# Decode attention on Trainium2: key-page products moved from VectorE to GpSimd, in place

## The chip, the cores and the metric

The kernel runs on one core of one Trainium2 chip. The metric is device time in microseconds (us) of one execution; lower is better. Engines are named as the profile names them: PE is TensorE's matmul, PEld its weight load, DVE is VectorE, ACT is ScalarE, POOL is GpSimd, and SP is SyncE, which here only issues transfers.

## The reference, cut to what matters

One decoder step of two layers over 512 prompt tokens and 8 sample tokens. Layer 0 is a recurrent mixer with a convolutional FFN, layer 1 differential attention with a convolutional FFN. The change is in layer 1's attention of the samples over their paged cache: each of 8 samples has 4 pages of 128 past keys, each key 1024 numbers (8 heads x 2 halves x 64).

```python
qs, ks, vs = att_project(hs, att_w_in[j], att_q_norm_g[j], att_k_norm_g[j])
past_k = cache_k[j, page_table].reshape(db_, past, A_HEADS, 2, A_QK_DIM)
past_v = cache_v[j, page_table].reshape(db_, past, A_HEADS, A_V_DIM)
...
s = jnp.einsum('bqhcd,bkhcd->bchqk', q, k) * A_QK_DIM ** -0.5   # q.k for each key, head and half
p = softmax(s); a = p[:, 0] - lam * p[:, 1]; out = a @ v
```

## The kernel before, in words

Everything is in one program. Each engine has its own block of instructions in an order written out by hand, and the engines meet only at semaphores: `Steps` (a named list of counts) turns the name of a step and a round number into a wait.

Layer 1's attention is done in 8 rounds of `head(h, ...)`, one such function on each of PE, ACT, DVE and POOL. Rounds 0 and 7 are written out, rounds 1 to 6 are a hardware loop of three passes of two. A round does two things at once: prompt head h (four blocks of 128 queries, k = 0 to 3, each attending to k+1 blocks of keys), and sample h (all its heads, over its 4 pages). In the same round PE multiplies the weights of the next head's keys and values (`part`, L557).

Prompt side of a round. PE makes the scores of block k (`s{k}`, L842). DVE's `stats(k)` adds the mask (L1851), takes the maximum (L1854) and scales it by a small `tensor_scalar` of two numbers per partition (`nx{k}`, L1856). ACT's `exps(k)` takes exponentials and sums (L1299, step `ex{k}`). DVE's `combine(k)` is four instructions: reciprocal (L1863), product of two-number rows (`rs`, L1865), `tensor_scalar` on the second half's exponentials (L1867), and the combination of both halves (`a{k}`, L1871). PE transposes that (`turn`, L850), ACT copies it (L1305), PE multiplies it with the values (L856).

Sample side. POOL spreads the sample's query over a diagonal (`qd`, L1996). PE multiplies it with ones (`qb`, L878), and ACT copies the result to `qb` in SBUF: the query row in every partition (L1311). SP loads the 4 pages of keys into `k_pages` (L439). For page j DVE's `page(j)` multiplies the page with `qb` into the buffer `s_prod` (128x1024, step `mul{j}`, L1881), and DVE's `scores(j)` sums the 64 numbers of each head and half (`red{j}`, L1886). Once `red3` is done PE transposes the scores (`st`, L912). `s_prod` is one buffer, so `mul{j}` waits for `red{j-1}`; the page's slot is free for sample h+1 once `mul{j}` is done.

DVE's order in a round is stats(0), combine(0), stats(1), page(0), combine(1), scores(0), stats(2), page(1), combine(2), scores(1), stats(3), page(2), combine(3), scores(2), page(3), scores(3), then the split of the next weight slab (`w_lo`, L1399) and the rest of the round.

POOL's order in a round is `qd` (it waits for PE's `qb` of the round before), the copy of the new keys (`ks`, L2084) and their transfer out (L2085), the copy of the new values (`vs`, L2090) and their transfer out (L2091). The `qd` of round h+1 is thus ready to run as soon as PE's `qb` of round h is done.

Of the kernel before, what the change touches and what calls it, by code (L numbers as in the profile page):

```python
# [29 lines left out]
P = 128  # L30
D_MODEL, T, B = 1024, 512, 8
# [3 lines left out]
M_HEADS, G_PAIRS, A_HEADS, A_QK = 4, 2, 8, 64  # L35
# [72 lines left out]
def build(nc, a):  # L108
    F32, F32R, I32 = mybir.dt.float32, mybir.dt.float32r, mybir.dt.int32
    ALU, ACT, AX = mybir.AluOpType, mybir.ActivationFunctionType, mybir.AxisListType  # L110
    V, S, G, TE = nc.vector, nc.scalar, nc.gpsimd, nc.tensor
    ds = bass.ds
    ctx = ExitStack()
    with ctx:
        END = 229344

        def place(name, shape, dt=F32, at=None):

            size = 4 * int(np.prod(shape[1:]))
            size += -size % 32  # L120
            assert at[0] + size <= END, (name, at[0] + size)
            t = nc.alloc_sbuf_tensor_at(name, shape, dt, offset=at[0])
            at[0] += size
            return t

        def sem(name):
            return ctx.enter_context(nc.semaphore(name))
# [13 lines left out]
        k_pages = place("k_pages", [P, PAGES, D_MODEL], at=[pages_at])  # L141
# [5 lines left out]
        at = [norm_at]  # L147
# [5 lines left out]
        at = [region]  # L153
# [14 lines left out]
        at = [work]  # L168
# [7 lines left out]
        at = [work]  # L176
# [20 lines left out]
        at = [region]  # L197
# [5 lines left out]
        at = [region + 12 * NT * 4]  # L203
# [4 lines left out]
        at = [rows_at]  # L208
# [3 lines left out]
        at = [work]  # L212
# [11 lines left out]
        at = [region]  # L224
# [10 lines left out]
        at = [region]  # L235
# [9 lines left out]
        ks = place("ks", [P, A_HEADS, B], at=at)  # L245
        vs = place("vs", [P, A_HEADS, B], at=at)
        qn = place("qn", [P, 2, NT], at=at)
        kn = place("kn", [P, 2, NT], at=at)
# [7 lines left out]
        s_sc = place("s_sc", [P, PAGES, 16], at=at)  # L256
# [7 lines left out]
        at_t = place("at_t", [P, 2, T], at=at)  # L264
        sq3 = place("sq3", [P, 3, NT], at=at)
        rs3 = place("rs3", [P, 3, NT], at=at)
        s_prod = place("s_prod", [P, D_MODEL], at=at)
        o_row = raw[:, 0, D_MODEL:D_MODEL + 2 * P]
        qb = place("qb", [P, D_MODEL], at=at)
        qd = place("qd", [P, A_HEADS, P], at=at)  # L270
        qs_r, qs_t = (qd[:, n, 0:A_HEADS * B].rearrange("p (h b) -> p h b", b=B) for n in range(2))

        at = [pages_at]
# [46 lines left out]
        k_in = [sem(f"k_in{i}") for i in range(PAGES)]  # L320
# [39 lines left out]
        def both(engine, names):  # L360

            last = " ".join(n for n in names.split() if n not in NEXT.split())
            return Steps(sem("att_" + engine), names), Steps(sem("last_" + engine), last)
        aP, zP = both("pe", "s0 qb s1 ssq t0 v0 s2 t1 v1 s3 t2 v2 t3 v3 st mb ssk sso vtr pv sum")
        aA, zA = both("act", "sqq ex0 qb att0 ex1 lrq rq att1 ex2 kr sqk att2 ex3 att3 sqo vr se lrk rk lro ro vt orow")
        aD, zD = both("dve", "m0 x0 nx0 r0 rc0 e0 a0 m1 x1 nx1 mul0 r1 rc1 e1 a1 red0 m2 x2 nx2 mul1 r2 rc2 e2 a2 red1 "
                      "m3 x3 nx3 mul2 r3 rc3 e3 a3 red2 mul3 red3 smax dmx qn msv sub ls kn mix lall")
        aG = Steps(sem("att_pool"), "qd ks vs")
        bP = Steps(sem("first_pe"), "sqs ssq ssk vtr")
        bA = Steps(sem("first_act"), "sqs lrs rqs sqq lrq rq kr sqk vr lrk rk vt")  # L370
        bD = Steps(sem("first_dve"), "qs qn kn")
# [12 lines left out]
        def wait(eng, steps, name, r=0):  # L384

            eng.wait_ge(steps.sem, steps.at(name, r))
# [7 lines left out]
        def _(sp):  # L394
# [40 lines left out]
            def load_page(cache, buf, landed_, b, j, free=None):  # L435
                page = sp.value_load(ptab[0:1, ds(PAGES * b + j, 1)], min_val=0, max_val=POOL - 1)
                if free is not None:
                    wait(sp, *free)
                sp.dma_start(buf[:, j, :], a[cache][page]).then_inc(landed_[j], 16)  # L439
# [24 lines left out]
            def sample_pages(h, slabs_):  # L464

                for j in range(PAGES):
                    load_page("cache_k", k_pages, k_in, h + 1, j, (aD, f"mul{j}", h))
                for s in range(2):
                    slabs_(s)
                for j in range(PAGES):  # L470
                    load_page("cache_v", v_pages, v_in, h + 1, j, (aP, "pv", h))
                store_past(h, aA, h)
# [3 lines left out]
            with sp.Fori(0, (A_HEADS - 2) // 2) as i:  # L476
                for w in range(2):
                    sample_pages(2 * i + (1 + w), lambda u: load_slab("att_kv", KT, i, 10 + 2 * w + u))
            wait(sp, zD, "mul3")
            load_past(0, B - 1)  # L480
            store_past(B - 1, zA, 0)
            load_past(B - 1, B)
# [911 lines left out]
        def _(dve):  # L1394
# [448 lines left out]
            def head(h, u, i, h0, last=False):  # L1843

                sP_, sA_, sD_, r = (zP, zA, zD, 0) if last else (aP, aA, aD, h)
# [25 lines left out]
                    V.scalar_tensor_tensor(out=a_att[:, b, w], in0=e_att[:, b, 0, w], scalar=rs[:, b, 0:1],  # L1871
                                           in1=e_att[:, b, 1, w], op0=ALU.mult, op1=ALU.subtract).then_inc(sD_.sem, 1)

                def page(j):

                    if j == 0:
                        wait(dve, sA_, "qb", r)
                    else:
                        wait(dve, sD_, f"red{j - 1}", r)
                    dve.wait_ge(k_in[j], 16 * h + 16)  # L1880
                    V.tensor_tensor(s_prod[:, :], k_pages[:, j, :], qb[:, :], ALU.mult).then_inc(sD_.sem, 1)  # L1881

                def scores(j):

                    wait(dve, sD_, f"mul{j}", r)
                    V.tensor_reduce(s_sc[:, j, :], s_prod[:, :].rearrange("p (h d) -> p h d", d=A_QK), AX.X,  # L1886
                                    ALU.add).then_inc(sD_.sem, 1)

                stats(0)
                combine(0)  # L1890
                stats(1)
                page(0)
                combine(1)
                scores(0)
                stats(2)
                page(1)
                combine(2)
                scores(1)
                stats(3)
                page(2)  # L1900
                combine(3)
                scores(2)
                page(3)
                scores(3)
                if not last:
                    split("att_kv", i, 2 * (h0 + 2), KT)
# [82 lines left out]
        def _(pool):  # L1989
# [78 lines left out]
            pool.wait_ge(slab_done, FIRST["att_q"])  # L2068
            pool.dma_start(catt[:, :], a["catt"]).then_inc(catt_in, 16)

            def head(h, u, first=False):

                if first:
                    wait(pool, bD, "qs")
                else:
                    wait(pool, aP, "qb", h - 1)
                row = qs[:, :, h] if isinstance(h, int) else qs[:, :, ds(h, 1)].rearrange("p h o -> p (h o)")
                spread(qd[:, :, :], row, A_HEADS).then_inc(aG.sem, 1)
                if first:
                    wait(pool, bD, "kn")  # L2080
                else:
                    wait(pool, aD, "kn", h - 1)
                one_head = slice(h, h + 1) if isinstance(h, int) else ds(h, 1)
                G.tensor_copy(ks[:, one_head, :], kn[:, u:u + 1, T:NT]).then_inc(aG.sem, 1)  # L2084
                pool.dma_start(a["o_k"][:, one_head, :], kn[:, u:u + 1, :]).then_inc(kn_out, 16)  # L2085
                if first:
                    wait(pool, bA, "vr")
                else:
                    wait(pool, aA, "vr", h - 1)
                G.tensor_copy(vs[:, one_head, :], vn[:, T:NT].rearrange("p (o b) -> p o b", o=1)).then_inc(aG.sem, 1)  # L2090
                pool.dma_start(a["o_v"][:, one_head, :], vn[:, :].rearrange("p (o t) -> p o t", o=1)).then_inc(vn_out, 16)  # L2091

            head(0, 0, True)
            with pool.Fori(0, (A_HEADS - 2) // 2) as i:
                for w in range(2):
                    head(2 * i + (1 + w), 1 - w)
            head(A_HEADS - 1, 1)


            pool.wait_ge(kn_out, 16 * A_HEADS)  # L2100
# [154 lines left out]
```

## Time and profile before

| | us |
|---|---|
| median of 3 runs | 1571.17 (1569.27 to 1573.22) |
| the profiled execution, its own time | 1572.7 |
| its span, first to last instruction | 1570.9 |
| PE busy | 1446.6 (92%) |
| DVE busy | 872.7 (56%) |
| ACT busy | 532.0 (34%) |
| POOL busy | 114.8 (7%) |
| the 8 attention rounds | about 865.9 to 1126.9 of the span |
| mean granted TensorE clock | 0.951 of full speed |

Times within the trace count from the span's start. Busy shares are means over stages with different limits; what the change is worth is read from the attention rounds alone.

### The profile page before, as it was taken

To read this page: it belongs to the slowest core of one execution; us is meant where nothing else is said; L and a number is where in the kernel's file an instruction comes from. 1 tells how busy PE (TensorE), PEld (TensorE's weight loads), DVE (VectorE), ACT (ScalarE), POOL (GpSimd) and SP (SyncE) were. 2 spreads that over 40 slices of the span, in tenths; PEclk is the share of its full clock that TensorE was granted. 3 is DMA by queue.
4 is the path that set the end of the run, shared out by engine and by line. 5 is a ranking of instruction groups with operands and counts; after the bars stand their busy time and mean duration, and the time that the engine had idled before them with its cause. 6 is when DMAs were issued, how large, how long until landed. Compare 5 with 4: busy or idle time off the path is not lost.

```text
span 1570.9 us, 29852 instructions
## 1 busy us (share of the span) xinstructions
PE 1446.6 (92%) x11889; PEld 1356.6 (86%) x11889; DVE 872.7 (56%) x1332; ACT 532.0 (34%) x857; POOL 114.8 (7%) x125
## 2 busy tenths in 40 slices
PE   5999998578999999999999888888599999999997
PEld 5889897458999999999999666666499999999997
DVE  5465456732466666633244778877645666665221
ACT  4323432422433332332233455455333333322110
POOL 0120112110100000001000110001010000000000
PEclk9899999658999999999999999999699999999999
DMA  5232122001222222332224464456022222233320
GB/s 193 76 101 83 56 91 87 17 30 54 71 92 93 93 93 93 105 104 92 77 83 170 141 217 169 166 174 208 31 81 90 86 93 93 93 98 113 113 87 20
DMA packets 42780, 158.34 MB, mean 101 GB/s; under 512 B 5162, under 2 KB 6490, under 8 KB 42458
## 3 DMA queue, kind: packets, MB, share of 16 engines
q1 hardware_dynamic: 38506, 143.77, 27.9%
q0 software_dynamic: 4208, 13.63, 2.4%
q8 instruction: 48, 0.79, 0.2%
q14 instruction: 18, 0.15, 0.0%
HBM read 145.98 MB, written 11.40 MB: 100 GB/s over the span
## 4 chain that ended last, share of the span: by engine, by line
PE 81%; DVE 10%; issue 4%; ACT 4%; POOL 0%; DMA 0%; DVEq 0%; ACTq 0%; POOLq 0%
PE ps L506 56%; PE ps L557 12%; DVE mx L1854 2%; DVE s_sc L1886 1%; PE ps L954 1%; ACT e_att L1299 1%; ACT w_hi L1023 1%; PE ps L606 1%; PE ps L930 1%; PE ps L878 1%; DVE e_att L1867 1%; DVE ps L1851 1%; PE ps L687 1%; DVE a_att L1871 1%; PE ps L856 1%
## 5 line engine op out<-in xcount | busy, mean ns | idle before, releaser
L506 PE MATMUL ps<-h_hi,w_hi 128*128 128x260 f32 x1744 | 498.6, 286 | 9.5 <-DVE h_lo L1408 4.6
L506 PE MATMUL ps<-h_hi,w_lo 128*128 128x260 f32 x1744 | 496.5, 285 | 0.0
L506 PE MATMUL ps<-h_lo,w_hi 128*128 128x260 f32 x1744 | 495.1, 284 | 0.0
L1399 DVE TENSOR_TENSOR w_lo<-raw,w_hi 128x1024 fp32r<-128x1024 f32 (+1 forms) x189 | 247.7, 1311 | 419.6 <-ACT w_hi L1023 419.6
L506 PEld LDWEIGHTS ps<-h_hi,w_hi 128*128 128x128 f32 x1744 | 332.3, 191 | 11.6 <-issue 9.4
L506 PEld LDWEIGHTS ps<-h_lo,w_hi 128*128 128x128 f32 x1744 | 332.2, 190 | 0.2
L506 PEld LDWEIGHTS ps<-h_hi,w_lo 128*128 128x128 f32 x1744 | 332.2, 190 | 0.0
L1023 ACT CAST w_hi<-raw 128x1024 fp32r<-128x1024 f32 (+1 forms) x189 | 208.1, 1101 | 239.9 <-PE ps L506 233.8
L506 PE MATMUL ps<-a_lo,w_hi 128*128 128x260 f32 x704 | 199.0, 283 | 0.0
L506 PE MATMUL ps<-a_hi,w_hi 128*128 128x260 f32 x704 | 198.7, 282 | 0.0
L506 PE MATMUL ps<-a_hi,w_lo 128*128 128x260 f32 x704 | 198.7, 282 | 0.0
L506 PEld LDWEIGHTS ps<-a_hi,w_lo 128*128 128x128 f32 x704 | 132.6, 188 | 0.0
L506 PEld LDWEIGHTS ps<-a_hi,w_hi 128*128 128x128 f32 x704 | 132.5, 188 | 0.0
L506 PEld LDWEIGHTS ps<-a_lo,w_hi 128*128 128x128 f32 x704 | 132.5, 188 | 0.0
L557 PE MATMUL ps<-h_hi,w_hi 128*128 128x260 f32 x384 | 117.2, 305 | 2.1 <-ACT z L1085 2.1
L557 PE MATMUL ps<-h_lo,w_hi 128*128 128x260 f32 x384 | 110.9, 289 | 0.0
L557 PE MATMUL ps<-h_hi,w_lo 128*128 128x260 f32 x384 | 110.8, 289 | 0.0
L557 PE MATMUL ps<-n_hi,w_hi 128*128 128x260 f32 x256 | 82.0, 320 | 0.0
L557 PEld LDWEIGHTS ps<-h_hi,w_hi 128*128 128x128 f32 x384 | 75.2, 196 | 5.6 <-ACT z L1085 3.8
L557 PEld LDWEIGHTS ps<-h_lo,w_hi 128*128 128x128 f32 x384 | 75.2, 196 | 1.3 <-issue 1.0
L557 PEld LDWEIGHTS ps<-h_hi,w_lo 128*128 128x128 f32 x384 | 75.0, 195 | 0.0
L557 PE MATMUL ps<-n_lo,w_hi 128*128 128x260 f32 x256 | 75.0, 293 | 0.0
(364 smaller groups left out, 2040.9 us busy)
## 6 DMA issues: line engine op xcount, KB each, us to landing
raw<-in_w_ffn SPq DMA_DIRECT2D x88, 512.0 KB, 3.4
raw<-in_w_down SPq DMA_DIRECT2D x32, 704.0 KB, 4.0
k_pages<-in_cache_k SPq DMA_DIRECT2D x32, 512.0 KB, 3.5
v_pages<-in_cache_v SPq DMA_DIRECT2D x32, 512.0 KB, 6.3
raw<-in_w_rec_in SPq DMA_DIRECT2D x29, 512.0 KB, 3.5
raw<-in_w_att_kv SPq DMA_DIRECT2D x24, 512.0 KB, 3.5
raw<-in_w_rec_out SPq DMA_DIRECT2D x8, 512.0 KB, 3.4
raw<-in_w_att_q SPq DMA_DIRECT2D x8, 512.0 KB, 3.4
```

The source lines that it names most:

```text
L506: ins = TE.matmul(half(bank, h), w_part[:, buf, w], m_part[:, k_at + k, h * HALF:(h + 1) * HALF], start=start, stop=stop)
L557: ins = TE.matmul(half(bank, g), w_part[:, buf, w], m_part[:, k, g * HALF:(g + 1) * HALF], start=k == 0 and w_part is w_hi and m_part is h ...
L606: TE.matmul(ps[:, bank, :], SEL[0:4, h, :], row[:, :], start=True, stop=True).then_inc(mP.sem, 1)
L687: ins = TE.matmul(ps[o, at_bank + hh, w], key, lev[r, lv, t], start=True, stop=True)
L856: ins = TE.matmul(ps[:, 5, i * P:(i + 1) * P], v_t2[:, u, c, :], at_t[:, i % 2, c * P:(c + 1) * P], start=c == 0, stop=c == i)
L878: ins = TE.matmul(ps[:, 6 + g, :], ONES, qd[:, 4 * g:4 * g + 4, :].rearrange("p h k -> p (h k)"), start=True, stop=True)
L930: ins = TE.matmul(ps[32 * g:32 * g + 4, 6, 0:2 * P], s_sc[:, j, 4 * g:4 * g + 4], v_pages[:, j, 2 * P * g:2 * P * (g + 1)], start=j == 0, ...
L954: ins = TE.matmul(half(2 * s, g), w_part[:, (f_out + s) % 2, w], m_part[:, k, g * HALF:(g + 1) * HALF], start=k == 0 and w_part is w_hi an ...
L1023: S.copy(w_hi[:, n % 2, 0:nk * P], raw[:, n % RAW, 0:nk * P]).then_inc(hi_split, 1)
L1299: ins = S.activation(e_att[:, k % 2, c, 0:(k + 1) * P], ps[:, 2 + c, 0:(k + 1) * P], ACT.Exp, bias=mx[:, k % 2, c:c + 1], scale=A_QK ** -0 ...
L1399: V.tensor_tensor(w_lo[:, n % 2, 0:nk * P], raw[:, n % RAW, 0:nk * P], w_hi[:, n % 2, 0:nk * P].bitcast(F32), ALU.subtract).then_inc(lo_sp ...
L1854: V.tensor_reduce(mx[:, k % 2, :], s[:, :, 0:(k + 1) * P], AX.X, ALU.max).then_inc(sD_.sem, 1)
```

## The change

The product of a page with the query is made by POOL, and written over the page itself. DVE's `page(j)` and the buffer `s_prod` go; DVE's `scores(j)` waits for POOL's `mul{j}` and sums over the page. SP's load of page j of the next sample waits for DVE's `red{j}` instead of `mul{j}`, since the page now holds the products. On POOL the order in a round becomes qd, ks copy, transfer, page(0), page(1), vs copy, transfer, page(2), page(3).

```diff
-        s_prod = place("s_prod", [P, D_MODEL], at=at)
...
-        aG = Steps(sem("att_pool"), "qd ks vs")
+        aG = Steps(sem("att_pool"), "qd ks mul0 mul1 vs mul2 mul3")
...
                 for j in range(PAGES):
-                    load_page("cache_k", k_pages, k_in, h + 1, j, (aD, f"mul{j}", h))
+                    load_page("cache_k", k_pages, k_in, h + 1, j, (aD, f"red{j}", h))
...
-                def page(j):
-
-                    if j == 0:
-                        wait(dve, sA_, "qb", r)
-                    else:
-                        wait(dve, sD_, f"red{j - 1}", r)
-                    dve.wait_ge(k_in[j], 16 * h + 16)
-                    V.tensor_tensor(s_prod[:, :], k_pages[:, j, :], qb[:, :], ALU.mult).then_inc(sD_.sem, 1)
-
                 def scores(j):
 
-                    wait(dve, sD_, f"mul{j}", r)
-                    V.tensor_reduce(s_sc[:, j, :], s_prod[:, :].rearrange("p (h d) -> p h d", d=A_QK), AX.X,
+                    wait(dve, aG, f"mul{j}", h)
+                    V.tensor_reduce(s_sc[:, j, :], k_pages[:, j, :].rearrange("p (h d) -> p h d", d=A_QK), AX.X,
                                     ALU.add).then_inc(sD_.sem, 1)
...
-            def head(h, u, first=False):
+            def head(h, u, first=False, last=False):
+
+                def page(j):
+                    if j == 0:
+                        if last:
+                            wait(pool, zA, "qb")
+                        else:
+                            wait(pool, aA, "qb", h)
+                    pool.wait_ge(k_in[j], 16 * h + 16)
+                    G.tensor_tensor(k_pages[:, j, :], k_pages[:, j, :], qb[:, :], ALU.mult).then_inc(aG.sem, 1)
...
                 pool.dma_start(a["o_k"][:, one_head, :], kn[:, u:u + 1, :]).then_inc(kn_out, 16)
+                page(0)
+                page(1)
...
                 pool.dma_start(a["o_v"][:, one_head, :], vn[:, :].rearrange("p (o t) -> p o t", o=1)).then_inc(vn_out, 16)
+                page(2)
+                page(3)
```

## Rows read from the trace of the kernel before

**Rows 1.** Page, chain that ended last, share of the span by engine.
```profile
PE 81%; DVE 10%; issue 4%; ACT 4%; POOL 0%; DMA 0%; DVEq 0%; ACTq 0%; POOLq 0%
```

**Rows 2.** The chain in order of time, round 3: start us, us, what.
```profile
965.75 1.72 PE ps L878 x4
...
985.17 0.66 PE ps L850 x4
...
988.89 0.60 PE ps L912 x4
...
997.83 1.72 PE ps L878 x4
```

**Rows 3.** Timeline of DVE, round 3: start us, us, instruction, [idle before <-releaser].
```profile
970.76 0.17 DVE L1856 TENSOR_SCALAR mx<-mx 128x2 f32<-128x2 f32 x1
970.96 1.23 DVE L1881 TENSOR_TENSOR s_prod<-k_pages,qb 128x1024 f32<-128x1024 f32 x1
972.10 0.16 DVE L1863 RECIPROCAL rs<-sm 128x2 f32<-128x2 f32 x1
...
973.28 1.21 DVE L1886 TENSOR_REDUCE s_sc<-s_prod 128x16 f32<-128x1024 f32 x1
...
977.32 0.17 DVE L1863 RECIPROCAL rs<-sm 128x2 f32<-128x2 f32 x1
...
987.54 1.22 DVE L1886 TENSOR_REDUCE s_sc<-s_prod 128x16 f32<-128x1024 f32 x1
```

**Rows 4.** Timeline of ACT, round 3, same columns.
```profile
967.50 1.01 ACT L1311 COPY qb<-ps 128x1024 f32<-128x1024 f32 x1 [1.31 <-PE ps L878]
...
971.79 0.20 ACT L1299 ACTIVATION_READ_ACCUMULATOR e_att<-ps,mx 128x1 f32 x1
...
977.09 0.20 ACT L1299 ACTIVATION_READ_ACCUMULATOR e_att<-ps,mx 128x1 f32 x1
```

**Rows 5.** Timeline of POOL, round 3, the values' transfer out.
```profile
964.13 0.54 POOL L2091 DMA_DIRECT2D out_o_v<-vn  x1
```

**Rows 6.** Page, DMA issues: count, KB each, median us from issue to landing.
```profile
k_pages<-in_cache_k SPq DMA_DIRECT2D x32, 512.0 KB, 3.5
```

**Rows 7.** POOL's products by line: duration ns min/median/max, first and last start us, forms.
```profile
L1390 POOL TENSOR_TENSOR ge<-ge,sq x21: 1301/1352/1368, 384.5 to 1186.2; 128x520 f32<-128x520 f32 x21
...
L1996 POOL TENSOR_TENSOR qd<-cst,qs x8: 1908/1911/1912, 853.8 to 1065.0; 128x1024 f32<-128x1024 f32 x8
```

**Rows 8.** DVE and POOL at once in layer 0 (timeline), and L1399's durations.
```profile
87.37 0.15 DVE L1615 COPY n_end<-c_n 128x1 f32<-128x1 f32 x1
...
111.24 1.89 POOL L1996 TENSOR_TENSOR kv<-cst,z 128x1024 f32<-128x1024 f32 x1 [9.29 <-PE ps L606]
111.70 2.50 DVE L1399 TENSOR_TENSOR w_lo<-raw,w_hi 128x1024 fp32r<-128x1024 f32 x1 [3.93 <-ACT w_hi L1023]
113.31 2.66 POOL L1992 TENSOR_TENSOR c_s<-c_s,w_s 128x1024 f32<-128x1024 f32 x1 [0.17 <-ACT w_s L1140]
...
265.88 3.76 POOL L1996 TENSOR_TENSOR g_dv<-cst,z 128x1024 f32<-128x1024 f32 x2
266.39 4.35 DVE L1670 SCALAR_TENSOR_TENSOR g_h<-log_a 128x1040 f32<-128x1040 f32 x1
...
L1399 DVE TENSOR_TENSOR w_lo<-raw,w_hi x189: 1160/1225/2505, 12.7 to 1548.6; 128x1024 fp32r<-128x1024 f32 x157, 128x1408 fp32r<-128x1408 f32 x32
```

**Rows 9.** Groups of DVE by form, attention rounds: busy us, mean ns | idle before.
```profile
L1871 DVE SCALAR_TENSOR_TENSOR a_att<-e_att,rs 128x512 f32<-128x512 f32 x8 | 6.0, 751 | 0.8
...
L1867 DVE TENSOR_SCALAR e_att<-e_att,rs 128x512 f32<-128x512 f32 x8 | 3.9, 486 | 0.6 <-DVE rs L1865 0.3
```

**Rows 10.** Clock: a stretch of round 5 (PEclk eighth), chain pieces of rounds 5, 4.
```profile
1050.00:1053.00 3.00, 3.00 (x18) 3.00 (x17) 2.93 (x4) 0.58 (x1) 0.00 (x0) 0.61 0.20 51
...
1050.55 3.02 PE ps L557 x18
...
1017.88 2.16 PE ps L557 x18
```

More of the change, by code:

```diff
@@ L365, in build @@
         aA, zA = both("act", "sqq ex0 qb att0 ex1 lrq rq att1 ex2 kr sqk att2 ex3 att3 sqo vr se lrk rk lro ro vt orow")
-        aD, zD = both("dve", "m0 x0 nx0 r0 rc0 e0 a0 m1 x1 nx1 mul0 r1 rc1 e1 a1 red0 m2 x2 nx2 mul1 r2 rc2 e2 a2 red1 "
-                      "m3 x3 nx3 mul2 r3 rc3 e3 a3 red2 mul3 red3 smax dmx qn msv sub ls kn mix lall")
-        aG = Steps(sem("att_pool"), "qd ks vs")
+        aD, zD = both("dve", "m0 x0 nx0 r0 rc0 e0 a0 m1 x1 nx1 r1 rc1 e1 a1 red0 m2 x2 nx2 r2 rc2 e2 a2 red1 "
+                      "m3 x3 nx3 r3 rc3 e3 a3 red2 red3 smax dmx qn msv sub ls kn mix lall")
+        aG = Steps(sem("att_pool"), "qd ks mul0 mul1 vs mul2 mul3")
         bP = Steps(sem("first_pe"), "sqs ssq ssk vtr")
@@ L478, in _ @@
                     sample_pages(2 * i + (1 + w), lambda u: load_slab("att_kv", KT, i, 10 + 2 * w + u))
-            wait(sp, zD, "mul3")
+            wait(sp, zD, "red3")
             load_past(0, B - 1)
@@ L1891, in head @@
                 stats(1)
-                page(0)
                 combine(1)
@@ L1895, in head @@
                 stats(2)
-                page(1)
                 combine(2)
@@ L1899, in head @@
                 stats(3)
-                page(2)
                 combine(3)
                 scores(2)
-                page(3)
                 scores(3)
@@ L2096, in _ @@
                     head(2 * i + (1 + w), 1 - w)
-            head(A_HEADS - 1, 1)
+            head(A_HEADS - 1, 1, last=True)
             pool.wait_ge(kn_out, 16 * A_HEADS)
```

## The prediction

> **What bounds the kernel now.** I read the page's chain first: PE carries four fifths of it over the whole span [rows 1]. That mean says little about the attention rounds, so I read the chain in order of time through one middle round, then each engine's timeline of the same stretch. A round lasts 997.83 - 965.75 = 32.1 us [rows 2], and it has two halves. From PE's qb product to 985.17, where PE turns the last block, the chain runs DVE, ACT, DVE: maximum of a block, exponentials, combination, next block. From 985.17 to the next round PE works without a gap, so the chain is PE's. A delay of DVE in the first half reaches the end one for one; free DVE time in the second half is worth nothing.
>
> **What goes.** Four DVE products per round, each 1.23 us [rows 3], 32 in all, 39 us of DVE's time. What lies on the path is much less.
> - Page 0 stands between stats(1) and combine(1). Combine(1) starts at 972.10, but it needs ex1, which ACT finishes at 971.79 + 0.20 = 971.99 [rows 3, 4]. With the product gone it starts near 972.03: 0.07 us gained.
> - Page 1 lies under ACT's exponentials, which end at 977.09 + 0.20 = 977.29; combine(2) starts at 977.32 [rows 3, 4]. Nothing gained. Page 2 lies under the next, longer, exponentials in the same way.
> - Page 3 goes after combine(3). Its sum ends at 987.54 + 1.22 = 988.76, and PE's transpose of the scores, next in PE's order, starts at 988.89 when PE is through with its own work [rows 2, 3]. Nothing gained; the next thing late is PE itself.
> The gain is 8 x 0.07 = 0.6 us. The cover in all four cases is ACT's exponentials or PE's queue.
>
> **What moves.** SP's loads of the next sample's pages wait for the sum, some 1.2 us later than for the product. The slab loads queued behind them on SP wait for the split of w_lo, which DVE makes after the last sum anyway. A page lands 3.5 us after its issue [rows 6] and is wanted after the next round's qb, so nothing is late: zero. POOL's copy of vs and its transfer come after two products; ACT wants them only for the next values in the second half, over ten us later: zero. POOL's qd of the next round comes after four products; PE wants it a round later: zero.
>
> **What comes: the products' own time on POOL.** No row shows this product on POOL. The nearest rows are 520 elements of two plain inputs in 1.30 to 1.37 us, and 1024 elements with spread-out inputs in 1.91 us [rows 7]. The ends are 1.91 and 1.30 x 1024/520 = 2.56 us. I take 2.39, nearer to the plain product, since both inputs here are plain and a part of its 1.30 us is fixed (I take 0.17, what the smallest instruction of [rows 3] takes, and scale the rest). The Trainium skill (GPSIMD Engine Reference, section 3.1) gives 4497 ns for 2048 elements; half of that, an estimate, is 2.25 us and would shorten the sum below by 5%. POOL starts at 968.55, when ACT's copy of qb is done (967.50 + 1.01) [rows 4]. Two products end at 973.3, the vs copy (eight numbers, 0.2 as an estimate from the 0.15 of the one-number copy in [rows 8]) and the issue of the transfer (0.54) [rows 5] at 974.0, two more products at 978.8, and qd, ready since long, at 980.7. The sums on DVE ask for the first product at 973.3 and for the last at 987.5 [rows 3], so if it were a matter of time alone, POOL would be early even at (987.5 - 968.55 - 0.75)/4 = 4.5 us a product.
>
> **What comes: two engines at one port.** This is the term that decides. In layer 0 DVE's split w_lo, with two SBUF inputs, takes 1.23 us alone. Started at 111.70 behind a POOL product that ran from 111.24 to 113.13, it took 2.50 us: it stood until 113.13 and then took its usual time. The POOL product that started at 113.31 then stood in turn, 2.66 us instead of 1.9 [rows 8]. So a DVE instruction with two SBUF inputs and a POOL product exclude each other for a whole instruction. Where two POOL products followed each other without a wait between (265.88, 3.76 us for both), DVE's instruction of 266.39 got in only after the second: 4.35 us, ending at 270.7, for what is little over a microsecond of work [rows 8]. DVE is not let in between. The copy of one number at 87.37 ran in 0.15 us beside a POOL product [rows 8], so not every DVE instruction is held.
> The Trainium skill (SBUF — State Buffer, Who interferes with whom) says the same: DVE's second SBUF read port is POOL's, taken by whoever starts first for the whole instruction, by two SBUF inputs and also by two-port modes of tensor_scalar. By that rule nx1 (L1856) is held as well, the first case below rather than the second; no run here shows it.
>
> In the first half of a round these DVE instructions stand on the path while POOL is busy: the rs product (two SBUF inputs) and the combination (two SBUF inputs) of combine(1) and combine(2); perhaps L1867, which does 512 numbers in 486 ns where the combination needs 751 [rows 9], so it moves more than one at a time and may use both read paths; and L1856, of the same kind. POOL's stretch has two blocks with no wait left between their instructions: products 0 and 1, 968.55 to 973.3, then, behind the short issue, products 2, 3 and qd, 974.0 to 980.7.
> Combine(1)'s second instruction would start at 972.3. It stands until 973.3 at least. Then 0.5 to 0.7 us are left, and combine(1) from its reciprocal to the sum's start takes 973.28 - 972.10 = 1.2 us [rows 3], 1.0 of it behind the reciprocal; if L1856 was held too, the exponentials (1 us) come ahead of it. I take it that one misses, and stands behind the second block: 980.7 - 972.3 = 8.4 us. Behind 980.7 POOL is silent, and blocks 2 and 3 run as before. Eight rounds: 67 us. With 1.91 and 2.56 us a product the block ends at 978.8 or 981.4: 6.5 or 9.1 us a round, 52 to 73 us.
>
> **The clock.** PE would stand for over 8 us a round. In round 5 PE stood 2.9 us and then ran at a granted clock of 0.61 (mostly the 1.2 GHz level), and 18 matmuls took 3.02 us instead of 2.16 [rows 10]. Most of PE's slower work would lie beside DVE's chain and before 985 of the old count; I take 0.5 us a round (0 to 1.4), 4 us.
>
> **Sum.** The profiled execution's own time is 1572.7 us (span 1570.9 and 1.8 around it). 1572.7 - 0.6 + 67 + 4 = 1643. It lies 1.5 us above the median of the runs, so the forecast is 1642.
>
> **Rivals.**
> 1. DVE gets through once: combine(1) finishes in the gap between POOL's blocks (a loss of about 1 us), and only combine(2) meets the second block, which then ends at 981.1 as it was itself held. Its second instruction would start at 977.5, so 3.6 us a round, 29 us, and 3 for the clock: 1603 (with 1.91 us a product near 1590). Letting DVE in at every POOL boundary ends within 1 us a round of this, since qd still falls on combine(2). For it: the gap exists, and a waiting DVE was let in at 113.13. Against: three instructions must fit in it.
> 2. The products cost far more, as POOL is held too by DVE's instructions or by in-place operands: from 4.5 us a product on, red3 is late for PE also. At 3.2 us a product the block ends at 984: 11.7 us a round, 1667.
> 3. No change. The small instructions of combine are not held, or POOL lets DVE in at once. Then 0.6 us is gained: 1570.6. For it: the one-number copy. Against: the rows of exclusion are exact to 0.1 us.
> 4. Faster: the DVE time removed is on the path. The chain charges page 0 with 1.1 us, and page 3 is 1.2 us before the score transpose; if ACT's ex1 and PE's queue moved up along with DVE, 2.3 us a round, 19 us: 1552. It decides only where ex1 is done before 971 and PE is free before 987.6; ex1's end at 971.99 and PE's unbroken work speak against it.
>
> **How the numbers follow.** Forecast 0.50, rival 1 0.30, rival 2 0.08, rival 3 0.09, rival 4 0.03. The forecast's own range is 1624 to 1655. The range to hold 8 in 10 takes in rival 1 down to its cheap product: 1590 to 1662. A measurement here tells some 0.3% (4.7 us) from no change. Faster 0.03, same 0.07 (rival 3, less its worse edge), slower 0.90.
>
> **What would show it.** POOL products near 2.4 us in the rounds, in two unbroken blocks. Long rs (L1865), L1867, L1871 or L1856 rows in blocks 1 and 2, ending when a POOL instruction ends, and none in block 3. PE's wait for a_att grown by 4 or 8 us a round; rounds of 36 or 41 us. The forecast is wrong if the durations of those rows don't change, or if page loads or POOL are waited for by the sums.

## The result and the profile after

The changed kernel takes 1634.9 us (median of 4, 1633.9 to 1639.2), the kernel before on the same chip 1570.9. The ratio is 1.0414, with 1.0399 to 1.0429 as its 95% interval: slower by 64 us. The profiled execution took 1634.69 us; its span is 1633.0, 62.1 longer than before.

The page of the changed kernel: the busy time of each engine, then the chain's share by engine.
```profile
PE 1459.1 (89%) x11889; PEld 1366.9 (84%) x11889; DVE 893.3 (55%) x1300; ACT 532.6 (33%) x857; POOL 189.2 (12%) x157
...
PE 78%; DVE 11%; issue 6%; ACT 4%; POOL 0%; DMA 0%; DVEq 0%; ACTq 0%; POOLq 0%
```
DVE gave up 32 products, 39 us, and is busy for longer than it was (872.7 us before). What it is busy with is standing: a held instruction counts as busy. On the chain "issue" went from 4% [rows 1] to 6%.

Round 3 of the changed kernel, the chain in order of time (start us, us, what); it answers to [rows 2]. The wait rows after it give us in total, times and longest us: the first is the changed kernel's, the second that of the kernel before.
```profile
985.24 1.72 PE ps L877 x4
...
993.60 6.67 issue
...
1012.12 0.66 PE ps L849 x4
1012.77 3.31 PE ps L556 x18
...
1026.16 1.72 PE ps L877 x4
```
```profile
PE ps L849 <- DVE a_att L1870: 81.5, 21, 7.7
```
```profile
PE ps L850 <- DVE a_att L1871: 23.3, 23, 3.1
```
The round is 1026.16 - 985.24 = 40.9 us, 8.8 more than before. One piece of 6.67 us, in which the chain finds nothing but issue, is new.

POOL in the same round, timeline (start us, us, instruction), answering to [rows 5]:
```profile
988.18 4.69 POOL L2066 TENSOR_TENSOR k_pages<-k_pages,qb 128x1024 f32<-128x1024 f32 x2 [4.69 <-ACT qb L1310]
992.81 0.20 POOL L2087 COPY vs<-vn 128x8 f32 x1
992.94 0.58 POOL L2088 DMA_DIRECT2D out_o_v<-vn  x1
993.54 4.64 POOL L2066 TENSOR_TENSOR k_pages<-k_pages,qb 128x1024 f32<-128x1024 f32 x2
998.14 1.91 POOL L1982 TENSOR_TENSOR qd<-cst,qs 128x1024 f32<-128x1024 f32 x1
```
and DVE beside it, answering to [rows 3]:
```profile
990.26 0.30 DVE L1855 TENSOR_SCALAR mx<-mx 128x2 f32<-128x2 f32 x1
991.66 0.17 DVE L1862 RECIPROCAL rs<-sm 128x2 f32<-128x2 f32 x1 [1.09 <-ACT e_att L1298]
991.86 1.03 DVE L1864 TENSOR_TENSOR rs<-rs,coef 128x2 f32<-128x2 f32 x1
992.92 0.35 DVE L1866 TENSOR_SCALAR e_att<-e_att,rs 128x256 f32<-128x256 f32 x1
993.31 7.03 DVE L1870 SCALAR_TENSOR_TENSOR a_att<-e_att,rs 128x256 f32<-128x256 f32 x1
1000.26 1.21 DVE L1876 TENSOR_REDUCE s_sc<-k_pages 128x16 f32<-128x1024 f32 x1
...
1004.31 0.17 DVE L1862 RECIPROCAL rs<-sm 128x2 f32<-128x2 f32 x1 [1.30 <-ACT e_att L1298]
```
The two lists are read against each other by ends. The rs product of combine(1) ends at 992.89, when POOL's second product does (988.18 + 4.69 = 992.87). The combination L1870, 0.48 us of work, ends at 1000.34 after 7.03 us; POOL's second block ends with qd at 1000.05. Between them L1866 ran in its usual time in the gap that POOL's copy and its transfer leave. The first product ended near 990.53, and L1855 was held there for 0.13 us.

The same over all eight rounds, groups of DVE by form (busy us, mean ns | idle before):
```profile
L1870 DVE SCALAR_TENSOR_TENSOR a_att<-e_att,rs 128x256 f32<-128x256 f32 x8 | 54.4, 6798 | 0.3
...
L1864 DVE TENSOR_TENSOR rs<-rs,coef 128x2 f32<-128x2 f32 x32 | 12.1, 379 | 1.1
```
Unheld, in the kernel before, these take 484 and 160 ns on average; the first alone is 8 x 6.3 = 50 us.

### The profile page after: what moved, and what is told of

It is laid out like the page before. It is cut to its first block, busy times and chain, and to the rows that moved or that the text cites. A ratio compares the mean times of both kernels' runs of the same rounds, so it can differ in the third digit from the quotient of the medians.

```text
span 1633.0 us, 29810 instructions
## 1 busy us (share of the span) xinstructions
PE 1459.1 (89%) x11889; PEld 1366.9 (84%) x11889; DVE 893.3 (55%) x1300; ACT 532.6 (33%) x857; POOL 189.2 (12%) x157
## 4 chain that ended last, share of the span: by engine, by line
PE 78%; DVE 11%; issue 6%; ACT 4%; POOL 0%; DMA 0%; DVEq 0%; ACTq 0%; POOLq 0%
PE ps L505 54%; PE ps L556 12%; DVE mx L1853 1%; ACT e_att L1298 1%; DVE a_att L1870 1%; DVE s_sc L1876 1%; PE ps L953 1%; ACT w_hi L1022 1%; PE ps L929 1%; PE ps L877 1%; PE ps L605 1%; DVE rs L1864 1%; PE ps L855 1%; DVE e_att L1866 1%; PE ps L798 1%
## 5 line engine op out<-in xcount | busy, mean ns | idle before, releaser
L505 PEld LDWEIGHTS ps<-h_lo,w_hi 128*128 128x128 f32 x1744 | 331.0, 190 | 0.2
L505 PEld LDWEIGHTS ps<-h_hi,w_lo 128*128 128x128 f32 x1744 | 331.0, 190 | 0.0
L849 PEld LDWEIGHTS ps<-cst,a_att 128*128 128x128 f32 x80 | 9.8, 160 | 98.5 <-DVE a_att L1870 98.3
L849 PE MATMUL ps<-cst,a_att 128*128 128x128 f32 x80 | 18.2, 333 | 81.5 <-DVE a_att L1870 81.5
L556 PE MATMUL ps<-n_hi,w_hi 128*128 128x260 f32 x256 | 86.8, 339 | 0.0
L556 PE MATMUL ps<-n_lo,w_hi 128*128 128x260 f32 x256 | 79.5, 311 | 0.0
```

The source lines that it names most:

```text
L505: ins = TE.matmul(half(bank, h), w_part[:, buf, w], m_part[:, k_at + k, h * HALF:(h + 1) * HALF], start=start, stop=stop)
L556: ins = TE.matmul(half(bank, g), w_part[:, buf, w], m_part[:, k, g * HALF:(g + 1) * HALF], start=k == 0 and w_part is w_hi and m_part is h ...
L849: ins = TE.transpose(ps[:, 4, c * P:(c + 1) * P], a_att[:, i % 2, c * P:(c + 1) * P], IDENT)
```

## Where the 62 us lie

Round 3 was cut at the same places in both traces.

| stretch | before | after | difference |
|---|---|---|---|
| qb product to combine(1)'s reciprocal | 972.10 - 965.75 = 6.35 | 991.66 - 985.24 = 6.42 | +0.07 |
| that reciprocal to the end of combine(1), the sum's start | 1.18 | 1000.26 - 991.66 = 8.60 | +7.42 |
| that sum to combine(2)'s reciprocal | 4.04 | 4.05 | +0.01 |
| combine(2)'s reciprocal to PE's turn of block 3 | 7.85 | 7.81 | -0.04 |
| turn of block 3 to the next qb | 12.66 | 14.04 | +1.38 |

The second line is rs (+0.87) and the combination (+6.55). The last is PE working more slowly (its granted clock is shown further down): the 18 products behind the turn take 3.31 us instead of 2.16. Over all rounds, from the first qb to the eighth, the timelines of PE, before and then after, say:
```profile
867.86 1.88 PE L878 MATMUL ps<-qd,cst 128*128 128x512 f32 x4
...
1093.89 1.96 PE L878 MATMUL ps<-qd,cst 128*128 128x512 f32 x4 [0.22 <-DVE l_all L1934]
```
```profile
862.44 1.88 PE L877 MATMUL ps<-qd,cst 128*128 128x512 f32 x4
...
1147.70 1.95 PE L877 MATMUL ps<-qd,cst 128*128 128x512 f32 x4 [0.25 <-DVE l_all L1920]
```
That is 226.0 and 285.3 us, 59.2 more in seven rounds. The eighth round and what follows hold 62.1 + 5.4 - 59.2 = 8.3 more. The 5.4 is a difference ahead of the change: the first round begins 5.4 us earlier here. In the twelve traces of this study it begins anywhere from 861.4 to 868.9, whichever kernel it is, so a term of this size can't be told from the scatter of what runs ahead.

## Experiments

All are read against the kernel before, run on the same chip; ratios come with their 95% interval.

**Is it presence, or is it waiting for results?** In this kernel POOL makes its products as in the change, but DVE sums fixed numbers of another tensor, and only the reduction at the end of a round waits for POOL. SP's loads of the next pages wait for that reduction. The samples' scores are left out thereby.
```diff
-                    load_page("cache_k", k_pages, k_in, h + 1, j, (aD, f"red{j}", h))
+                    load_page("cache_k", k_pages, k_in, h + 1, j, (aD, "smax", h))
...
-                    wait(dve, aG, f"mul{j}", h)
-                    V.tensor_reduce(s_sc[:, j, :], k_pages[:, j, :].rearrange("p (h d) -> p h d", d=A_QK), AX.X,
+                    V.tensor_reduce(s_sc[:, j, :], fixed.rearrange("p (h d) -> p h d", d=A_QK), AX.X,
...
+                wait(dve, aG, "mul3", h)
```


> The changed kernel with POOL's four products in their places and sizes, but nobody's result: DVE's sums run over a fixed 128x1024 tensor and don't wait for POOL; only the end of the round waits for mul3 (left out of the output: the sample's true scores). Theory (two engines at one SBUF port, the presence of POOL's products alone): as the changed kernel, 1635 +- 4, L1870's 128x256 form again near 6.8 us and L1864 near 1 us in block 1. Rival (the sums wait for late products, a matter of data): back to 1570 to 1575, L1870's 128x256 form at 0.48 us.

Measured: 1637.1 us, ratio 1.0416 (1.0397 to 1.0434), the same as the change. Its group of DVE:
```profile
L1871 DVE SCALAR_TENSOR_TENSOR a_att<-e_att,rs 128x256 f32<-128x256 f32 x8 | 54.4, 6802 | 0.3
```
No wait of the sums and no late page carries any of the 64 us. POOL's products cost them by being there.

**Does it take a POOL instruction that reads?** Each product is replaced by one of 8 numbers and two memsets, of 1016 and 300 numbers, that only write; together they keep POOL busy for about 1.5 us. The sums and the loads are as in the run before; the products and scores are left out.
```diff
-                    G.tensor_tensor(k_pages[:, j, :], k_pages[:, j, :], qb[:, :], ALU.mult).then_inc(aG.sem, 1)
+                    G.tensor_tensor(k_pages[:, j, 0:8], k_pages[:, j, 0:8], qb[:, 0:8], ALU.mult)
+                    G.memset(k_pages[:, j, 8:D_MODEL], 0.0)
+                    G.memset(more[:, j, :], 0.0).then_inc(aG.sem, 1)
```


> As the run nodep, but each product is replaced by a tiny 8-number product and two memsets (1016 and 300 numbers), so POOL is busy some 1.5 us a page and mostly only writes. Theory (the held DVE instructions want the read path that POOL reads through): block 1's L1864 at 0.16 us and L1870 at 0.48 us, since qd, which reads, starts only after combine(1): 1570 to 1577; L1855, if the write path matters, may stay a little long. Rival (any POOL instruction holds them): L1870 stands until qd's end, some 5 us a round, 1605 to 1615.

Measured: 1612.2 us, ratio 1.0241 (1.0212 to 1.0270). The time is the rival's; the trace is neither's alone. POOL and DVE of this kernel, round 3, put together by start:
```profile
986.82 0.94 POOL L2069 MEMSET k_pages<- 128x1016 f32 x1
987.43 0.63 DVE L1857 TENSOR_SCALAR mx<-mx 128x2 f32<-128x2 f32 x1
987.70 0.34 POOL L2070 MEMSET more<- 128x300 f32 x1
...
988.84 0.96 POOL L2069 MEMSET k_pages<- 128x1016 f32 x1
989.35 0.16 DVE L1866 TENSOR_TENSOR rs<-rs,coef 128x2 f32<-128x2 f32 x1
989.55 1.52 DVE L1868 TENSOR_SCALAR e_att<-e_att,rs 128x256 f32<-128x256 f32 x1
989.72 0.36 POOL L2070 MEMSET more<- 128x300 f32 x1
990.04 1.08 POOL L2068 TENSOR_TENSOR k_pages<-k_pages,qb 128x8 f32<-128x8 f32 x1
991.07 0.93 POOL L2069 MEMSET k_pages<- 128x1016 f32 x1
991.10 3.34 DVE L1872 SCALAR_TENSOR_TENSOR a_att<-e_att,rs 128x256 f32<-128x256 f32 x1
...
992.26 1.90 POOL L1984 TENSOR_TENSOR qd<-cst,qs 128x1024 f32<-128x1024 f32 x1
```
Four rows are to be told apart.
- rs, two SBUF inputs, ran in its usual 0.16 us in the middle of a memset. Beside a product it took 1.03.
- L1857, the tensor_scalar that scales the maximum, took 0.63 us instead of 0.17. Up to 987.99 only memsets ran beside it, and it ended with the second of them (988.06 against 988.04). So memsets do hold this form, which the change never showed.
- L1868, also a tensor_scalar, took 1.52 us instead of 0.35, and the 8-number product, 0.19 us elsewhere, stood along with it. How much of that is the memsets' is open: in the last round no memset ran beside it, only the transfer of vs and then an 8-number product, and it took 1.51.
- L1872 took 3.34 us, to the end of qd, though only memsets (the second at 991.95, 0.34 us) ran in its first 1.16 us. In the last round, also beside a memset but without qd behind, it took 0.48. Why it was not through before qd began stays open.

The Trainium skill (SBUF — State Buffer, Who interferes with whom) says that two SBUF inputs contend only with POOL instructions that read, and that the two-port modes of tensor_scalar contend with any POOL instruction. The trace agrees on the first point (0.16 us) and on the second (0.63 us). It does not explain the 3.34 us.

**Keep POOL out of one stretch.** Page 2's product waits for combine(1)'s last step, so the second block can't start ahead of it.
```diff
+                    if j in (2,):
+                        wait(pool, zD if last else aD, "%s" % {2: 'a1'}[j], 0 if last else h)
```


> The changed kernel, one wait added: POOL's page(2) waits for DVE's a1, so combine(1) can't fall behind POOL's second block; the block falls on combine(2) instead. Theory: L1870 128x256 at about 0.5 us; in block 2 L1864 stands some 2.4 us behind qd; a round is 3.4 us (with up to 1.3 for the clock) longer than before: 1597 to 1612. Rival (the loss follows POOL's total work, not where it falls): 1635.

Measured: 1593.8 us, ratio 1.0140 (1.0121 to 1.0159): 41 of the 64 us are gone, and the time is 3 us under the range that was expected. POOL and DVE of this kernel in block 2 of round 3:
```profile
978.84 4.68 POOL L2068 TENSOR_TENSOR k_pages<-k_pages,qb 128x1024 f32<-128x1024 f32 x2 [0.37 <-DVE a_att L1870]
981.24 2.30 DVE L1855 TENSOR_SCALAR mx<-mx 128x2 f32<-128x2 f32 x1
983.47 1.91 POOL L1982 TENSOR_TENSOR qd<-cst,qs 128x1024 f32<-128x1024 f32 x1
```
The combination takes 0.48 us in all rounds, and the block moved onto block 2's instructions. I had expected rs (L1864) there to stand 2.4 us behind qd. It stood 0.2; the maximum's scaling, L1855, was caught first, for 2.13 us, and was let in at 983.5, between the fourth product and qd. The two make 2.3 us, nearly what was expected, so this is not what brought the time below the range. A round is 35.15 us (1005.34 - 970.19), 3.1 more than before where 3.4 was expected, and PE's 18 products behind the turn of block 3 took 2.15 to 2.17 us in all seven rounds, where the kernel before has two slower ones (3.27 and 3.02). Over the kernel each of these two makes some 2 us.

**Keep POOL out of all of them.** Pages 1, 2 and 3 wait for the last step of combine(1), (2) and (3).
```diff
+                    if j in (1, 2, 3):
+                        wait(pool, zD if last else aD, "%s" % {1: 'a1', 2: 'a2', 3: 'a3'}[j], 0 if last else h)
```


> The changed kernel with POOL's page(1), page(2), page(3) waiting for DVE's a1, a2, a3: each product lies where DVE has only PSUM operands or sums to do. Theory: no long L1864, L1866, L1870 rows, at most 0.3 us a round lost (L1855 of block 1, w_lo behind qd): 1570 to 1575, verdict same as before. Rival (POOL's product is costly wherever it lies, or page 3 comes late for the score transpose): 1 us a round or more, 1580 and up.

Measured: 1573.2 us, ratio 1.0021 (1.0006 to 1.0035), as expected: 62 of the 64 us are gone. The products of pages 1 to 3 now run while DVE sums a page or works on scores in PSUM; page 0's still holds L1855, for 0.12 us. So nearly the whole loss was a matter of which DVE instructions POOL stood beside. What is left, in this kernel's round 3:
```profile
1015.90 1.91 POOL L1982 TENSOR_TENSOR qd<-cst,qs 128x1024 f32<-128x1024 f32 x1
1017.11 1.78 DVE L1398 TENSOR_TENSOR w_lo<-raw,w_hi 128x1024 fp32r<-128x1024 f32 x1
```
The gated products push qd onto the split of w_lo, which is held for 0.55 us. The round lasts 32.7 us (1026.77 - 994.06), 0.6 more than before: page 3's product starts only behind combine(3), and the last sum, w_lo and the row maximum follow it and come late for PE. And though 39 us of DVE's products are gone, nothing is gained.

**How much of it is qd?** In the change alone, qd waits for DVE's dmx of its round, far behind the block.
```diff
+                    wait(pool, aD, "dmx", h - 1)
```


> The changed kernel with POOL's qd waiting for DVE's dmx, late in the round, so that the block behind which combine(1) stands is products 2 and 3 alone. Theory (the block is held through all its instructions, qd's 1.91 us among them): L1870's 128x256 form falls from 6.8 to some 5.1 us, 1.9 us a round in seven rounds come back, 13 us: 1618 to 1625. Rival (combine(1) isn't held by qd, or qd holds other DVE work as dearly at its new place): 1632 and up.

Measured: 1616.1 us, ratio 1.0286 (1.0264 to 1.0308), about 2 us below what was expected. The combination's group:
```profile
L1870 DVE SCALAR_TENSOR_TENSOR a_att<-e_att,rs 128x256 f32<-128x256 f32 x8 | 41.4, 5172 | 0.3
```
From 6798 ns to 5172: 13.0 us in all, 1.86 in each of the seven rounds that have a qd, which is qd's own 1.91. The instruction stands behind exactly what POOL has queued without a wait. PE gives the rest: the 18 products take 2.15 to 2.17 us in all seven rounds of this trace, 8.0 us less than in the change, and the 8 matmuls behind them 0.89 us instead of 1.29. From the first qb to the eighth the trace is 23.8 us shorter; 3.9 of that don't show in the time, as its first round began later by as much.

**Does PE's slower stretch come from its 7 us of standing?** Matmuls of 512 columns into a free bank are added ahead of PE's wait for combine(1), 16 of them in one kernel.
```diff
+                for _ in range(16):
+                    TE.matmul(ps[:, 4, :], ONES, par[:, 0:512], start=True, stop=True)
```


> The changed kernel with 16 extra products of 128x512 on PE (about 0.43 us each, their result overwritten) in front of turn(1), where PE stands nearly 8 us a round. Theory (a part of the loss is the clock that falls while PE stands): the 18 products behind turn(3), 3.3 us in every round of the changed kernel and 2.16 before, go back to 2.16 in most rounds, and 1.4 us a round come back: 1623 to 1630. Rival (the clock costs nothing on the path, or falls for the later 3 us wait alone): 1633 to 1638.

Measured: 1674.9 us, ratio 1.0673 (1.0653 to 1.0692), outside both ranges. What was added is far longer than the stand: in the trace the 16 matmuls are 32 records, two passes of 0.44 us each, and last 14.0 us (from 960.68). They run past the end of the stand and delay the round by themselves. It doesn't separate the causes. With 8 of them:

```diff
+                for _ in range(8):
+                    TE.matmul(ps[:, 4, :], ONES, par[:, 0:512], start=True, stop=True)
```


> As pe_busy with 8 extra products instead of 16: each is two matrix passes of 0.44 us, so they fill 7.0 of the 7.4 us that PE stands before turn(1) and don't run past it. Theory (the clock falls because of that long stand): the 18 products behind turn(3) go back from 3.3 to 2.16 us in most rounds, 1622 to 1628. Rival (it falls in the 3 us wait ahead of turn(3), as pe_busy's 0.50 behind 14 us of work suggests, by where the rounds fall in time): the 18 products stay at 3 us and more, 1632 to 1640.

Measured, with 8: 1637.4 us, ratio 1.0424 (1.0403 to 1.0445), the rival's time. Windows of both kernels show where the clock fell (us, busy PE, PEld, DVE, ACT, POOL, then granted clock, DMA share, GB/s). The changed kernel:
```profile
995.00:1000.00 5.00, 0.00 (x0) 0.00 (x0) 5.00 (x1) 0.00 (x0) 5.00 (x3) 0.63 0.00 0
1004.00:1008.00 4.00, 3.21 (x22) 2.38 (x23) 3.47 (x7) 2.68 (x6) 0.00 (x0) 1.00 0.10 40
1012.00:1015.00 3.00, 2.88 (x18) 2.88 (x19) 3.00 (x4) 0.59 (x1) 0.00 (x0) 0.73 0.25 45
```
and the one with 8 added:
```profile
985.00:1012.00 27.00, 22.05 (x114) 14.41 (x112) 19.09 (x29) 9.80 (x25) 11.88 (x7) 1.00 0.38 140
1012.00:1015.00 3.00, 2.40 (x11) 2.40 (x12) 3.00 (x4) 0.59 (x1) 0.00 (x0) 0.58 0.11 15
```
In the change PE's granted clock falls twice in a round. It is 0.63 in a stretch in which PE only stands behind the combination; from 1004 on it is 1.00 again. Then it is 0.73 behind the turn of block 3. The 0.63 and the 0.73 are means of stretches at the level of 2.4 GHz and at that of 1.2. With 8 added matmuls the first fall is gone, 1.00 from 985 to 1012, and the second comes all the same, 0.58, behind the 3 us wait ahead of the turn of block 3; the 18 products take 3.18 to 3.23 us in six of seven rounds. So the long stand, which was one of the two causes I put up, is not needed for the fall that costs time. PE waits there for 2.8 us in the kernel before, in the change, with 8 matmuls added and with qd late, and for 2.0 us where POOL is gated at page 2. Behind that wait the clock fell in 2 of 7 rounds before, in 7 of 7 in the change, and in 0 of 7 in the kernel gated at page 2 and in the one with qd late. What decides is not shown here.

**Can a better order use the time that is gained?** First with the products on DVE as before: each sum is moved out of the stretch that the chain charges. The order of DVE is then stats(2), sum 0, combine(2), stats(3), page 1, combine(3), and the rest behind it.
```diff
                 combine(1)
+                stats(2)
                 scores(0)
-                stats(2)
+                combine(2)
+                stats(3)
                 page(1)
-                combine(2)
+                combine(3)
                 scores(1)
-                stats(3)
                 page(2)
-                combine(3)
                 scores(2)
                 page(3)
```


> The kernel before, DVE keeping its products, only its order changed: stats(2) ahead of scores(0), stats(3) ahead of page(1) and scores(1), the rest behind combine(3). Theory (a control for the next run): two sums leave the path (2.2 us a round), but 6 us of products and sums now stand between combine(3) and the score transpose, which has 3.7 us of room: about 0 a round, 1567 to 1577. Rival (order alone is worth the gain): 1560 and below.

Measured: 1582.0 us, ratio 1.0077 (1.0060 to 1.0094), 0.8% slower and 5 us above what was expected. The last sum, which had 0.1 us to spare before PE's transpose [rows 2, 3], now ends 2.4 us after PE is ready for it, which takes back what the order had gained. That alone is the expected nothing: round 1 lasts 32.3 us (931.66 - 899.35), as rounds do in the kernel before. But in the other rounds PE works more slowly behind this new wait, and five of them last 33.6 to 34.0 us. In round 3, where the granted clock from 989 to 993 is 0.57:
```profile
990.01 2.60 PE ps L557 x12
```
These 12 products take 1.44 us in round 1 and in the kernel before. Most of the loss is thus the clock's, behind a wait that the order made. Other orders with the products on DVE were not tried.

Then the same idea with POOL's products, gated as above. The sums go where DVE waits for ACT's exponentials, and the maxima go through PSUM, so that L1855 (here L1856) has no SBUF input.
```diff
+                    top = ps[:, 7, 508:510] if k == 3 else ps[:, 2, 508:510]
-                    V.tensor_reduce(mx[:, k % 2, :], s[:, :, 0:(k + 1) * P], AX.X, ALU.max).then_inc(sD_.sem, 1)
+                    V.tensor_reduce(top, s[:, :, 0:(k + 1) * P], AX.X, ALU.max).then_inc(sD_.sem, 1)
-                    V.tensor_scalar(mx[:, k % 2, :], mx[:, k % 2, :], -(A_QK ** -0.5), None, ALU.mult).then_inc(sD_.sem, 1)
+                    V.tensor_scalar(mx[:, k % 2, :], top, -(A_QK ** -0.5), None, ALU.mult).then_inc(sD_.sem, 1)
...
                 stats(1)
+                scores(0)
                 combine(1)
-                scores(0)
                 stats(2)
                 combine(2)
+                stats(3)
                 scores(1)
-                stats(3)
                 combine(3)
```


> POOL's products gated as in gate_all, and the DVE time they free used: sum 0 under the exponentials of block 1, sum 1 under those of block 3, sums 2 and 3 behind combine(3); the maxima go through PSUM so that L1855 has no SBUF input. Theory (POOL's products are free where DVE wants neither of the shared paths; freed DVE time pays only where it shortens the chain): combine(3) ends 2.2 us earlier in a round, 0.6 of it is lost again as w_lo stands behind qd and the row maximum comes late for PE: 1552 to 1562, the first to beat the kernel before. Rival (POOL's products hold something I don't see, or page 3 comes late): 1568 and up.

Measured: 1555.0 us, ratio 0.9905 (0.9888 to 0.9922), 1% faster, as expected. POOL and DVE, then two rounds' starts of the chain, then what the sums wait for (us in total, times, longest):
```profile
965.69 2.38 POOL L2069 TENSOR_TENSOR k_pages<-k_pages,qb 128x1024 f32<-128x1024 f32 x1 [2.51 <-DVE a_att L1871]
966.99 0.16 DVE L1856 TENSOR_SCALAR mx<-ps 128x2 f32<-128x2 f32 x1
```
```profile
957.89 1.73 PE ps L877 x4
...
988.38 1.73 PE ps L877 x4
```
```profile
DVE s_sc L1877 <- POOL k_pages L2069: 12.5, 11, 1.4
```
The scaling reads PSUM and ran in 0.16 us in the middle of a product. The Trainium skill (SBUF — State Buffer, Who interferes with whom) has an instruction with at most one SBUF input outside the two-port modes as free of POOL; this row agrees. A round is 30.5 us, 1.6 less than before and 2.2 less than in the kernel with all pages gated. Of these 2.2 the maxima through PSUM give 0.1, L1855's hold; the order gives the rest. Now the 39 us that left DVE are worth something, since the sums had to be off the path as well. What is late now is POOL itself: the last sum waits for page 3's product, and w_lo (1.78 us, held by qd) and the row maximum come behind it.

**And with qd moved behind dmx in that version:**
```diff
+                    wait(pool, aD, "dmx", h - 1)
```


> As moved, with POOL's qd waiting for DVE's dmx, so that w_lo isn't held by it. Theory: 0.3 to 0.6 us a round better than moved: 1549 to 1559. Rival: qd now holds qn (L1899) or the second w_lo and gives it back: the same time as moved within 2 us.

Measured: 1553.3 us, ratio 0.9897 (0.9881 to 0.9914), 1.7 us less than the version without; the two intervals overlap, so this step itself isn't shown to gain. In the trace qd (978.53, 2.35 us) left the first split of w_lo alone and fell on the second, which took 1.68 us instead of 1.22, after standing itself behind DVE for 0.44. This is the fastest version of the study, 16 us under the kernel before on the same chip (1569.5).

## Why the prediction was right, step by step

The forecast was 1642 us with 1590 to 1662 around it, and the time is 1635. Its likeliest case is what happened. That the number lies so near owes something to luck: two terms of the sum were off by 7 us and by 4, in opposite directions.

- **What bounds the kernel: right.** DVE's delay in the first half reached the end one for one (the second line of the table), and freed DVE time in the second half brought nothing.
- **The gain of 0.07 us a round: fits.** The first stretch grew by 0.07, and L1855's delay is 0.13, so the rest of it shrank by 0.06.
- **What moves costs nothing: right.** Without any wait for the products the time was the same.
- **A product's price: right.** I took 2.39 us between 1.91 and 2.56; 32 products took 2.33 to 2.38, median 2.35. The estimate from the Trainium skill (GPSIMD Engine Reference, section 3.1), 2.25 us, was 4% low. (By it four products are 0.56 us shorter, which is 7% of the 8.4 us a round, and not the 5% that I wrote.)
- **Combine(1) misses the gap: right, with the wrong cut.** I had one instruction stand from 972.3 to 980.7 of the old count, 8.4 us. In the trace it was two: rs was held for 0.87 us up to the gap, L1866 used the gap, and only the combination met the second block, for 6.55. With 0.13 for L1855 and the 0.06 gained that is 7.49 us a round, not 8.4. Of the 0.9 between them 0.14 is POOL's block, which ended 14.81 us after the start of qb where I had 14.95. Another 0.6 is rs and L1866, which were through before it and needn't be done behind it. The last 0.2 is that the sum started 0.21 us behind qd's end, where unheld it starts 0.40 behind the start of the combination.
- **Eight rounds of it: mis-sized.** In the last round no qd is behind the products. There the combination took 5.18 us, L1864 1.00 and L1855 1.52, so it lost 6.8. The held term is 7 x 7.49 + 6.8 = 59.2 us where the forecast said 67 less the 0.6 of gain.
- **The clock: half right, size too small.** The clock does fall behind the long stand, and what runs at it lies beside DVE's chain, as forecast. The fall that costs time is another one, behind the 3 us wait ahead of the turn of block 3, which I did not have in mind; the long stand isn't its condition, as it came with the stand filled as well. It costs 1.38 us in round 3, against 0.5. Seven rounds lost 59.2 - 7 x 7.49 = 6.8 us beyond the held term, forecast 4 for eight. It is less than 7 x 1.38, since two of the seven rounds of before had the slower stretch as well.
- **The sum.** 59.2 held + 6.8 for the clock + 1.5 for the tail - 5.4 from the earlier start = 62.1. The forecast was 70.4 against the profiled execution: 66.4 held, 7.2 too high; 4 for the clock where it and the tail are 8.3, 4.3 too low; and nothing of the 5.4. The first and the last outweigh the second by the 8.3 us that the forecast lies too high.
- **The rivals.** Rival 1 was half seen: DVE did get through the gap, with one instruction too few; from there the loss is 6.5 us, not 1. The kernel gated at page 2 lies where rival 1 put the time, 1594 against 1590 to 1603, by another instruction than it named. Rivals 2, 3 and 4 fell: products at 2.35, rows that did change, a sum that didn't move PE.
- **What would show it: as written**, but that the long rows are in block 1 alone, as POOL's second block was through before combine(2), and L1867 (L1866 here) is none of them. PE's wait for a_att grew by 58 us, 7.3 a round.
- **"DVE is not let in between": half right.** It holds for the combination and not for L1855, as the last section shows.

## What to carry to other kernels

Before work goes to POOL, list the instructions of DVE that would run beside it and mark those with two SBUF inputs and the tensor_scalars over SBUF; if one of them is on the path, it can cost the whole run of POOL instructions queued without a wait, here 6.6 us for 0.5 us of work. Bind such POOL work with waits to the stretches in which DVE reduces or reads PSUM: that took 1635 us back to 1573. Then look at what those waits make late: here the last product, its sum and the split behind it became the end of the chain. Time freed on an engine is worth nothing until something that the chain charges is moved into it, and only then did the kernel gain, 1553 against 1570.

## What the runs showed of the hardware that was not expected

**What starts first by the trace doesn't always go first.** In the change the combination began at 993.31, 0.23 us ahead of the POOL product of 993.54, and yet stood through that product, the next and qd. The Trainium skill (SBUF — State Buffer, Who interferes with whom) gives the pair to whoever issues first. By that the combination should have run in its 0.48 us and POOL should have stood; the trace shows the opposite, and the measurement decides. The transfer that POOL was issuing at that moment (992.94 to 993.52) is not the reason by itself: in the kernel gated at page 2 the same instruction started in the middle of such a transfer (978.26, the transfer from 977.89 to 978.47) and took 0.48 us. Perhaps an instruction's start on DVE comes before its turn at the port; no run here shows that.

**Some forms are let in between two POOL instructions, others not.** The last round of the changed kernel, DVE and POOL:
```profile
1150.79 4.63 POOL L2066 TENSOR_TENSOR k_pages<-k_pages,qb 128x1024 f32<-128x1024 f32 x2 [3.91 <-ACT qb L1310]
1151.63 1.52 DVE L1855 TENSOR_SCALAR mx<-mx 128x2 f32<-128x2 f32 x1
...
1155.87 5.18 DVE L1870 SCALAR_TENSOR_TENSOR a_att<-e_att,rs 128x256 f32<-128x256 f32 x1
1156.11 4.64 POOL L2066 TENSOR_TENSOR k_pages<-k_pages,qb 128x1024 f32<-128x1024 f32 x2
```
The first product of the pair ends near 1150.79 + 2.32 = 1153.1, and L1855 ends at 1153.15: it got in between the two. The combination found the same kind of boundary near 1158.4 and stood until 1161.05, behind both. With memsets L1857 itself was not let in between: it stood from 987.43 over the end of the first near 987.7 to the end of the second. What decides (the form, the size, what POOL runs next) is open. The rows of the kernel before had only the second kind (4.35 us behind two instructions, [rows 8]), and I took it for the rule.

**Two short instructions that meet cost more than their work.** In the kernel with memsets L1868 (0.35 us of work) and the 8-number product (0.19) met behind a memset, which ended at 990.08, and both were through only at 991.1: 1.0 us for 0.54 us of work. In its last round they met behind a transfer, which ended at 1139.69, and were through at 1140.8. Where two long ones met, in layer 0, no such price shows: w_lo ended at 114.20, and the product behind it 1.8 us later, at 115.97, where 1.9 us is what it takes alone [rows 8].
